# Hybrid decoder layer in float32: five tiles of tokens in place of six

## What is computed

```python
h = rmsnorm(x, g_pre_mix)
z, q, k, v, glow, og = jnp.split(h @ w_in, SPLIT_IDX, axis=-1)      # 512, 256, 256, 512, 16, 512 columns
gk = jax.nn.log_sigmoid((glow @ w_gk2 + b_gk2).astype(jnp.float32)) / GLA_GATE_NORMALIZER
pool_out, pool_new = pool_mixer(z, pool_buf, start, w_pool, pool_scale)   # windows 2, 4, 8, 16
gla_out, gla_new = gla_mixer(q, k, v, gk, og, gla_state, gla_norm)        # 4 heads, causal, a running state
mix = jnp.concatenate([pool_out.astype(x.dtype), gla_out.astype(x.dtype)], axis=-1) @ w_o
x = x + rmsnorm(mix, g_post_mix)
f, conv_new = conv_ffn(rmsnorm(x, g_pre_ffn), conv_buf, w_up, w_conv, b_conv, w_down)   # d_ff 2816
x = x + rmsnorm(f, g_post_ffn)
x = x + (p.astype(x.dtype) @ w_ple) * jax.nn.sigmoid(x @ w_ple_gate)
```

## Time and profile before

| | us |
|---|---|
| median of 3 runs | 2663.58 |
| lowest and highest | 2661.97, 2663.98 |
| the profiled execution, its own time | 2661.27 |
| its span, first to last instruction | 2659.6 |
| TensorE busy | 2583.8 (97%) |
| VectorE busy | 1745.9 (66%) |
| ScalarE busy | 1352.2 (51%) |
| GpSimd busy | 319.5 (12%) |
| mean granted clock of TensorE | 0.989 |

### The profile page before, as it was taken

One profiled execution on the slowest core, in us unless ns is written; L12 is line 12 of the kernel. 1 busy time (PEld: TensorE's weight loads), 2 busy tenths in 40 slices (PEclk: granted clock), 3 DMA queues, 4 the chain that ended last, 5 costly groups with the idle time before them and its releaser, 6 DMA issues.

```text
span 2659.6 us, 41261 instructions
## 1 busy us (share of the span) xinstructions
PE 2583.8 (97%) x16510; PEld 2518.8 (95%) x16510; DVE 1745.9 (66%) x2555; ACT 1352.2 (51%) x2156; POOL 319.5 (12%) x590
## 2 busy tenths in 40 slices
PE   7979999999999999999999999999999999999998
PEld 6969999999999999999999999999999999899997
DVE  6667757667665676666567666656766664667865
ACT  4445554555444455544445554444564444466554
POOL 3210101120000212000021200002120000212000
PEclk9989999999999999999999999999999999999999
DMA  5235444234434323444432344343234434335564
GB/s 145 74 99 168 151 138 131 88 119 139 151 123 123 109 82 121 139 151 123 122 110 88 119 141 150 124 120 106 88 119 136 143 124 129 118 128 175 187 182 138
DMA packets 102371, 340.44 MB, mean 128 GB/s; under 512 B 10558, under 2 KB 18918, under 8 KB 102182
## 3 DMA queue, kind: packets, MB, share of 16 engines
q1 hardware_dynamic: 102182, 337.81, 40.2%
HBM read 327.46 MB, written 10.31 MB: 127 GB/s over the span
## 4 chain that ended last, share of the span: by engine, by line
PE 88%; DVE 6%; ACT 2%; issue 1%; DMA 1%; POOL 1%; SPq 0%; POOLq 0%; DVEq 0%
PE G L1626 27%; PE G L1627 27%; PE G L1628 27%; PE X L1685 2%; DVE w_lo L1147 2%; DVE mixed L1361 1%; PE X L1619 1%; PE X L1622 1%; DVE ffn_out L1435 1%; DVE h_lo L1373 1%; DMA stage<-in_w_up_units_dram 1%; PE X L1738 1%; PE X L1805 0%; PE X L1753 0%; ACT w_hi L737 0%
## 5 line engine op out<-in xcount | busy, mean ns | idle before, releaser
L1626 PE MATMUL G<-h_hi,w_hi 128*128 128x384 f32 (+2 forms) x3264 | 1069.8, 328 | 26.6 <-DVE w_lo L1147 11.4
L1628 PE MATMUL G<-h_lo,w_hi 128*128 128x384 f32 (+2 forms) x3264 | 1055.7, 323 | 0.0
L1627 PE MATMUL G<-h_hi,w_lo 128*128 128x384 f32 (+2 forms) x3264 | 1055.3, 323 | 0.0
L1147 DVE TENSOR_TENSOR w_lo<-stage,w_hi 128x1024 fp32r<-128x1024 f32 (+1 forms) x612 | 758.7, 1240 | 215.6 <-ACT w_hi L737 214.8
L737 ACT ACTIVATE w_hi<-stage 128x1024 fp32r<-128x1024 f32 (+1 forms) x612 | 636.9, 1041 | 434.5 <-DMA stage<-in_w_up_units_dram 247.0
L1626 PEld LDWEIGHTS G<-h_hi,w_hi 128*128 128x128 f32 x3264 | 620.7, 190 | 35.6 <-DVE w_lo L1147 13.6
L1627 PEld LDWEIGHTS G<-h_hi,w_lo 128*128 128x128 f32 x3264 | 621.1, 190 | 0.9
L1628 PEld LDWEIGHTS G<-h_lo,w_hi 128*128 128x128 f32 x3264 | 620.2, 190 | 0.0
L1626 PE MATMUL G<-y_hi,w_hi 128*128 128x384 f32 (+2 forms) x1056 | 346.3, 328 | 0.0
L1628 PE MATMUL G<-y_lo,w_hi 128*128 128x384 f32 (+2 forms) x1056 | 339.6, 322 | 0.0
L1627 PE MATMUL G<-y_hi,w_lo 128*128 128x384 f32 (+2 forms) x1056 | 339.5, 321 | 0.0
(11 more groups left out here) (228 smaller groups left out, 2716.6 us busy)
## 6 DMA issues: line engine op xcount, KB each, us to landing
stage<-in_w_up_units_dram SPq DMA_DIRECT2D x264, 512.0 KB, 3.5
stage<-in_w_in_units_dram SPq DMA_DIRECT2D x96, 512.0 KB, 3.5
stage<-in_w_down_units_dram SPq DMA_DIRECT2D x96, 448.0 KB, 3.3
stage<-in_w_o_units_dram SPq DMA_DIRECT2D x48, 512.0 KB, 3.4
stage<-in_w_down_units_dram SPq DMA_DIRECT2D x48, 512.0 KB, 3.5
stage<-in_w_gate_units_dram SPq DMA_DIRECT2D x48, 512.0 KB, 3.5
x_tok<-in_x_prompt_dram SPq DMA_DIRECT2D x14, 512.0 KB, 5.8
stage<-in_w_ple_units_dram SPq DMA_DIRECT2D x12, 512.0 KB, 3.4
```

Of the source, the lines that this page charges most:

```text
L1147: dve.tensor_tensor(w_lo[s][:, 0:parts, :], stage[s][:, 0:parts, :], exact(w_hi[s][:, 0:parts, :]), ALU.subtract).then_inc(lo_made, 1)
L1626: pe.matmul(ps[:, 0:w], l_hi, r_hi[:, 0:w], start=start, stop=False)
L1627: pe.matmul(ps[:, 0:w], l_lo, r_hi[:, 0:w], start=False, stop=False)
L1628: return pe.matmul(ps[:, 0:w], l_hi, r_lo[:, 0:w], start=False, stop=stop)
```

## The change

Five tiles: the first as before, then four of 448 prompt tokens, that is three chunks of 128 and a rest of 64. Every tile now has a rest of 64 columns (`REST`): the samples in the first, half a chunk in the others. What the code did for the samples alone (their transposes, `A_s`, scores up to level 4) it does for every rest, and for the half chunk up to level 32; the half chunk is a fourth piece of the state and of the output. Its output waits twice for a semaphore of TensorE's own (`fence`). The pieces' outputs use other PSUM banks (`OUT_BANKS`), and the second and third both stand after unit in 14. To make room, `w_hi` has three buffers (`HIS`), so `make_hi` waits for the end of unit n - 3, `make_hi(n + 3)` is gone, and several tensors share space: `gap` lies over `ffn_out`, which makes `make_gap` wait for GpSimd's additions, and `turned` over `cum`, with a wait in the second tile. The squares of the attention's output are taken in two parts, 384 columns ahead of the last piece.

```diff
-TILES = ((0, 256, NS), (256, 384, 0), (640, 384, 0), (1024, 384, 0), (1408, 384, 0), (1792, 256, 0))
+TILES = ((0, 256, NS), (256, 448, 0), (704, 448, 0), (1152, 448, 0), (1600, 448, 0))
-TM = 384
+TM = 448
+REST = 64
+HIS = 3
+STATE_BANKS, OUT_BANKS = (0, 1, 2, 4), ((0, 1), (2, 3), (0, 1), (3, 4))
...
                     act.wait_ge(landed[s], 16 * (n // SLOTS + 1))
-                    act.activation(w_hi[s][:, 0:parts, :], stage[s][:, 0:parts, :], ACT.Copy).then_inc(hi_made, 1)
+                    if n >= HIS:
+                        act.wait_ge(*end_tick(UNITS[n - HIS]))
+                    act.activation(w_hi[n % HIS][:, 0:parts, :], stage[s][:, 0:parts, :], ACT.Copy).then_inc(hi_made, 1)
...
                         if t == 0:
                             root_o(t)
-                            make_hi(n + 3)
...
             def make_gap(t, n):
                 if n == 0:
                     dve.wait_ge(*cum_made.at(t, 1))
+                if n < 2 and t:
+
+                    dve.wait_ge(*x_done_at(t - 1, 2 * n + 1))
...
-                    if small(t) and LEVELS[n] <= 4:
+                    if LEVELS[n] <= rest_level(t):
...
+                def fence(last, j):
+
+                    if n < P:
+                        rest_begun.did(last, t, j)
+                        pe.wait_ge(*rest_begun.at(t, j))
...
-                    if 13 <= m < 13 + chunks(t):
-                        out_chunk(t, m - 13)
+                    if m == 13:
+                        out_chunk(t, 0)
+                    if m == 14:
+                        out_chunk(t, 1)
+                        if half(t):
+                            out_chunk(t, 2)
+                    if m == 15 and half(t):
+                        out_chunk(t, 3)
```

More of the change, by code:

```diff
@@ L383, in small, with full, half, rest_level @@
             return TILES[t][2]
+        def full(t):
+            return P * chunks(t)
+        def half(t):
+            return TILES[t][1] % P
+        def rest_level(t):
+            return SLEN // 2 if small(t) else REST // 2
+        def piece_cols(t, c):
+            return slice(P * c, min(P * c + P, prompt(t)))
         def cols(c):
@@ L427, in level_whole @@
         def level_whole(ap, h, t):
-            w = width(t) if h <= 4 else prompt(t)
+            w = width(t) if h <= rest_level(t) else full(t)
             return ap[:, :, 0:w].rearrange("p d (n w) -> p d n w", w=2 * h)
@@ L1024, in _ @@
                     act.preload_act_table_set(LN_EXP)
-                    if chunks(u) == 3:
-                        copy_out(u, 2)
-                    if small(u):
+                    if half(u):
+                        copy_out(u, 3)
+                        square_out(u, full(u), width(u))
+                    else:
                         copy_small_out(u)
-                    square_out(u)
+                        square_out(u, 0, width(u))
                     if kind == "ple":
@@ L1675, in scores @@
             def scores(t, n):
-                nc_, np_ = chunks(t), prompt(t)
+                nc_, rest = chunks(t), slice(full(t), width(t))
                 first = 2 * (n % 2)
@@ L1752, in inside @@
                     for b in range(2):
-                        last = pe.matmul(X[first + b][:, cols(d)], v_tok[:, c, cols(2 * d + b)],
-                                         A[:, b, d * chunks(t) + c, :], start=start, stop=not start)
+                        weights = A[:, b, d * chunks(t) + c, :] if n == P else A_rest[:, b, d, :]
+                        last = pe.matmul(X[banks[b]][:, P * d:P * d + n], v_tok[0:n, c, cols(2 * d + b)], weights,
+                                         start=start, stop=not start)
                     return last
@@ L1893, in ple_out @@
                         pe.wait_ge(*p_lo_made.at(t, k))
-                ps = open_bank((t, "ple", 4 * half + q))
+                ps = open_bank((t, "ple", 4 * part + q))
                 for k in range(2):
-                    last = product(ps, t, w_hi[s][:, 4 * k + q, :], w_lo[s][:, 4 * k + q, :], p_hi[:, k, :], p_lo[:, k, :],
+                    last = product(ps, t, w_hi[hi_s][:, 4 * k + q, :], w_lo[s][:, 4 * k + q, :], p_hi[:, k, :], p_lo[:, k, :],
                                    k == 0, k == 1)
@@ L1909, in down_part @@
                         pe.wait_ge(*y_lo_made.at(t, first + k))
-                    last = product(ps, t, w_hi[s][:, k, :], w_lo[s][:, k, :], y_hi[:, first + k, :], y_lo[:, first + k, :],
+                    last = product(ps, t, w_hi[hi_s][:, k, :], w_lo[s][:, k, :], y_hi[:, first + k, :], y_lo[:, first + k, :],
                                    first + k == 0, first + k == NF - 1)
```

327 lines of the change are left out of this document (172 added, 155 removed).

## The result

The kernel with five tiles takes 2690.9 us (2689.3 to 2693.2), the one before 2663.2 in the same runs: ratio 1.0101, 95% interval 1.0089 to 1.0113. It is 27 us slower (0.0101 x 2663), and the forecast was 31.7 us faster. So 59 us have to be found. The span of the profiled execution is 2687.6 us, for 2659.6.

What follows compares the result with a forecast made beforehand. TensorE's time was taken to bound the kernel (busy 97% of the span). Products -32.4 us and everything else, small matmuls and waits included, +0.7 us made -31.7: 2663.6 to 2631.9, say 2632 us; range 2617 to 2649.

Steps and rivals of the forecast that it cites:

- Term 1: TensorE's products: 14,400 become 12,000, the 9600 of width 448 at 200.0 ns each; 2272.1 against 2304.5 us, -32.4 us.
- rival 4: The product's fixed part isn't saved: 448 columns take 202.8 ns, 26.4 us of the gain missing, 2658 us; chance 0.03.
- Term 2: More small matmuls per tile of 448 than of 384 (scores, transposes, state, output of the rest): +10.7 us a tile.
- The rest output: Output of the rest in each wide tile: 0.3 to 0.5 us for each wait, together 2.3 us.
- Term 3: TensorE's waits: -2.0 us per tile of 448 behind a tile of 448; in the first tile +4 and +1.0 once.
- Up 3 of the first tile: First tile's third up unit: the copy now lies on the path to TensorE's wait of 3.73 us, +1.0 us.
- The first tile's gates: Gates still 320 wide beside a 448-wide `norm_step`: +3 us of uncovered VectorE work and +1 for the clock, +4 once.
- the wait before `make_diag`: TensorE's 1.24 us wait for VectorE ahead of the attention shrinks by about 0.5 us and doesn't vanish.
- 1: Rival: the waits go altogether, with the clock's fall before the attention, and the gates' waits halve; 2620 us; chance 0.14.
- 2: Rival: at the two hand-overs VectorE and GpSimd are slower than by width, with a second low-clock stretch; 2648 us; chance 0.14.
- 3: Rival: three `w_hi` buffers expose copy and subtraction, 46 us at five places in each wide tile, 2678 us; chance 0.05.
- 5: Rival: the change doesn't do what it says, a DMA or a bank holds the rest back; given no chance of its own.

Runs made afterwards that it cites:

- experiment 5: Five-tile kernel with 64 bytes free behind the weights' high parts: ratio 0.9994 to the kernel before, against 1.0101; kernel before with 128 bytes: 1.0081.
- experiment 6: Five-tile kernel with the first tile's two whole-chunk outputs back in banks 3, 4 and 0, 1: ratio 1.0064 to the kernel before.
- experiment 9: Kernel before (six tiles) with three buffers of high parts in place of four, without the early third rounding in the first tile: ratio 1.0012.

## Why the prediction was wrong

**Term 1, the products, is the step that failed.** Three widths on one line were taken to carry on to a fourth. The trace of before couldn't contradict it: 256, 320 and 384 are on the line, 512 would have been, and 448 is not, in the place where these buffers lie. The term was put at 200.0 ns a product and -32.4 us; the products took 202.7 ns, in places 206.7, and 28.5 us of the gain were missing (experiment 5). The number of rival 4 was right (202.8 forecast, 202.7 measured), and at 0.03 it had far too small a chance for something that no row showed and on which every ns is worth 9.6 us. Its mechanism was wrong: the fixed part is not bound to what a product does, since the same products have 200.0 with 64 bytes between the buffers. The 2.5 ns of the Trainium skill (TensorE: Matmul & The Clock Gate, section Back-to-back issue gap) pointed the same way, and the trace agrees with it at no width.

**Term 2, the small matmuls, was short by about 15 us** over four tiles. The transposes of the rests were priced from six 128 x 128 ones, 0.11 us; x and p are turned with 64 rows, and 40 of them cost 0.38: 10.8 us more by TensorE alone, 7.5 with an interval of 5 or 6 either way by the layer's time. The scores cost 14.7 for 11.2. Both errors are one: a group's price was read from its own rows, and the change of mode stands between the rows of two groups. The rest output was right: units in 14 and 15 together grew by 2.2 us in a wide tile, for 2.3.

**Left out altogether:** the first tile's output banks, 7.5 to 10 us. The new table `OUT_BANKS` was in the diff, and the order of TensorE alone doesn't tell who frees a bank. VectorE's `mask_kd`, 6.6 us in front of `next_state`, was in the trace.

**Term 3, the waits, came out; the clock did not.** Up 3 of the first tile: 4.68 us for 3.73, +0.95 for a forecast of +1.0, and 1 to 2 us more behind it at the lower clock. The first tile's gates: the gate units grew by 3.7 us, for +4. In the third tile the wait before `make_diag` is gone (1.24 us; 0.7 was forecast to stay). The waits around the last gates are 2.93 us for 0.82 + 1.52 + 1.33 = 3.67, so -0.7 for a forecast of -1.0, and the one ahead of ple 0 (0.53) is gone, as forecast. That is 2.5 us less of waits for the 2.0 of the prediction, though it had let VectorE's work grow by a seventh, and 448 is a sixth more than 384. But the low clock behind `make_diag` stayed: it now falls behind a stretch of small matmuls alone. And behind the last gates three tiles have a stretch at the lower clock where one had it before: 5.1 us in place of 2.6. No experiment isolates this part; it is read from single executions, and in that of experiment 6 two wide tiles have such a stretch, not three.

**Rivals.** 1: the wait before `make_diag` went, but the clock fell behind it anyway, and the gates' waits didn't halve. 2: its second stretch at the lower clock came, its longer waits didn't. 3: out (experiment 9), 3 us in place of 46. 5: out.

**The account:** 28.5 for the pace, 8 to 10 for the banks, 8 to 11 for the 64-row turnings, 3.5 for the scores, 1 to 2 for up 3, 2 to 3 for the clock behind the last gates: 51 to 58 of 59 us. The first four rest on experiments, the last two are read from traces. Of what is left over, the fourth piece of the state has some (by starts in the fourth tile it costs 1.3 us for the 0.9 of term 2); the rest stays open. With the first three mended and part of the scores' price, the kernel is at 0.9913, or 23 us under; the forecast was 31.7.

The range (2617 to 2649) failed for the same reason as the number: it allowed for the doubtful terms and nothing for the one that seemed certain.

## What to carry to other kernels

When a change brings a shape that the profile has never shown, put both ends on its unit time and multiply by the count before looking at anything else: 2.7 ns times 9600 outweighed all the waits together. Read what matmuls cost from unit to unit (product before to product after), not from their own rows, since a change between 64-row, 64 x 64 and 128-row modes hides between them; padding 64 rows to 128 was cheaper than changing (0.11 us for 0.38). And a matmul stream with no wait in the profile can still lose 1.5% (384 columns) or 3% (448) by where its buffers start: at these widths the streamed operand 64 bytes past the weights was the best or as good as any.

## What was new about the chip

- The distance in memory between the streamed operand and the weights, within 256 bytes, sets the pace of back-to-back fp32r products: 448 columns 200.0 ns at 64 bytes, 202.2 at 192, 202.7 or 206.7 at 0, 204.0 at 128; 384 columns 173.3, but 175.9 at 128 (and once 176.7 at 192); 320 always 146.7. For these four distances the weights were moved as well as the streamed operand. The Trainium skill has two independent read ports for the two (TensorE: Matmul & The Clock Gate, section Step-by-step: what each phase is for), by which the places shouldn't matter; the measurement decides. By what mechanism they do is open: nothing here tells the memory's banks from the order of requests.
- At distance 0, 448 columns have two paces, 202.7 and 206.7 ns, that hold for hundreds of products. With TensorE alone what stood before chose between them; in the layer one kernel had the slower one for whole stages in one execution, and that execution was 9.5 us over the median of the five.
- 512 columns run at 226.8 ns, 13.5 above width / 2.4: per column 0.8% better than 448 at its best place and 2% better than at 202.7.
- Going to a transpose of 64 rows and back costs 0.27 us, a second one in a row 0.06. One that takes 128 rows and gives 64 costs nothing beside one of 128 x 128.
